# Embedding rows turned behind the first half tiles of the third output stage; the last stage's stores issued by SP, half a tile at a time

## What is computed

```python
def second_block(x, p, ...):
    h = x
    for i in range(DEPTH_2):                      # DEPTH_2 = 1
        xn = rms_norm(h, mix_norm[i])
        z = xn @ w_in[i]
        q, k, v, gate_a, u, gate_s = jnp.split(z, splits, axis=-1)
        attn = dilated_mixture_attention(q, k, v, q_norm[i], k_norm[i]) * jax.nn.silu(gate_a)
        ssm = s5_glu(u, ...) * jax.nn.silu(gate_s)
        h = h + jnp.concatenate([attn, ssm], axis=-1) @ w_out[i]
        gate = jax.nn.sigmoid(rms_norm(h, ple_norm[i]) @ w_ple_gate[i])
        h = h + gate * (p[i] @ w_ple_proj[i])
    return h
```

## Time and profile before

| | us |
|---|---|
| median of 3 runs | 2830.58 |
| lowest and highest run | 2827.45 and 2832.51 |
| the profiled execution, its own time | 2830.81 |
| span of that execution | 2829.0 |
| TensorE busy (PE) | 2726.1, 96% of the span |
| VectorE busy (DVE) | 1069.9, 38% |
| ScalarE busy (ACT) | 785.7, 28% |
| GpSimd busy (POOL) | 223.7, 8% |
| mean granted TensorE clock | 0.992 of full speed |

### The profile page before, as it was taken

One profiled execution on the slowest core, in us unless ns is written; L12 is line 12 of the kernel. 1 busy time (PEld: TensorE's weight loads), 2 busy tenths in 40 slices (PEclk: granted clock), 3 DMA queues, 4 the chain that ended last, 5 costly groups with the idle time before them and its releaser, 6 DMA issues. The chain is left out here.

```text
span 2829.0 us, 32445 instructions
## 1 busy us (share of the span) xinstructions
PE 2726.1 (96%) x12154; PEld 1529.1 (54%) x12154; DVE 1069.9 (38%) x3023; ACT 785.7 (28%) x1684; POOL 223.7 (8%) x409
## 2 busy tenths in 40 slices
PE   5999999999999999999999999999999999999998
PEld 3477544477644445466745476444654465644443
DVE  3257521299712223344400174123833473212211
ACT  3136400277711112322200264112211462111100
POOL 2000000000000000000060030200000002012000
PEclk8999999999999999999999999999999999999999
DMA  7030000012011220211010001333220204134311
GB/s 261 7 109 32 20 30 30 30 68 72 34 65 65 79 86 19 93 38 38 12 54 30 30 22 42 86 83 119 96 71 30 71 16 133 67 119 168 133 60 45
DMA packets 71867, 188.46 MB, mean 67 GB/s; under 512 B 6844, under 2 KB 9600, under 8 KB 70784
## 3 DMA queue, kind: packets, MB, share of 16 engines
q0 software_dynamic: 27808, 99.04, 10.8%
q1 hardware_dynamic: 43152, 86.97, 8.9%
q10 hardware_dynamic: 752, 0.38, 0.0%
HBM read 143.69 MB, written 43.01 MB: 66 GB/s over the span
## 5 line engine op out<-in xcount | busy, mean ns | idle before, releaser
L1305 PE MATMUL psum<-RW,hT 128*128 128x512 f32 (+2 forms) x2208 | 926.2, 575 | 7.5 <-ACT hT L2197 4.7
L1305 PEld LDWEIGHTS psum<-RW,hT 128*128 128x128 f32 x2208 | 428.0, 198 | 434.8 <-issue 412.8
L1271 PE MATMUL psum<-RW,RQ 128*128 128x512 f32 x832 | 362.3, 594 | 1.1 <-ACT RQ L2234 1.1
L1341 PE MATMUL psum<-RQ 64*128 64x256 f32 (+5 forms) x1344 | 291.7, 492 | 2.3 <-DVE small L2038 1.5
L2383 ACT ACTIVATE RP<-RP,small 128x1280 f32<-128x1280 f32 (+11 forms) x274 | 252.0, 920 | 131.0 <-DVE small L2038 127.0
L2038 DVE CUSTOM_DVE_ANT_0 RP<-psum,small 128x512 f32<-128x512 f32 (+1 forms) x382 | 201.5, 574 | 178.5 <-PE psum L1341 89.7
L1271 PEld LDWEIGHTS psum<-RW,RQ 128*128 128x128 f32 x832 | 157.0, 191 | 191.4 <-issue 191.4
L1353 PE MATMUL psum<-ident,RP 128*128 128x128 f32 x1388 | 203.7, 281 | 9.8 <-DVE RP L2051 4.5
L2395 ACT ACTIVATE RP<-psum 128x512 f32<-128x512 f32 (+1 forms) x288 | 150.1, 521 | 192.0 <-PE psum L1353 180.3
L1353 PEld LDWEIGHTS psum<-ident,RP 128*128 128x128 f32 x1388 | 149.4, 141 | 81.7 <-issue 67.9
L1341 PEld LDWEIGHTS psum<-RQ 64*128 64x128 f32 (+1 forms) x1344 | 139.2, 186 | 90.4 <-issue 48.9
(11 more groups left out here) (321 smaller groups left out, 2284.3 us busy)
## 6 DMA issues: line engine op xcount, KB each, us to landing
RW<-in_w_in SPq DMA_DIRECT2D x7, 2048.0 KB, 8.1
RW<-in_ev_w_in SPq DMA_DIRECT2D x6, 2048.0 KB, 8.1
RW<-in_od_w_ada SPq DMA_DIRECT2D x6, 2048.0 KB, 7.9
RW<-in_od_w_in SPq DMA_DIRECT2D x5, 2048.0 KB, 7.9
RQ<-in_ev_w_ada SPq DMA_DIRECT2D x4, 2048.0 KB, 21.0
RX<-in_x POOLq DMA_DIRECT2D x16, 512.0 KB, 6.0
y_even<-YR POOLq DMA_DIRECT2D x20, 256.0 KB, 2.3
RP<-y_even POOLq DMA_DIRECT2D x20, 256.0 KB, 3.0
```

The costliest lines, as they stand in the source:

```text
L1271: last = pe.matmul(main.bank(f), yT[:, kk, :], w_buf(n)[:, kk, :], start=kk == 0, stop=kk == KC - 1)
L1305: last = pe.matmul(main.bank(f)[:, 0:nc_], lhs_of(st["lhs"], j["t"], kk), w, start=kk == 0, stop=kk == kn - 1)
L1341: last = pe.matmul(main.bank(f)[:, 0:pc["w"]], q, kk[:, keys], start=i == 0, stop=i == len(u["qk"]) - 1)
```

## The change

The two loads get semaphores of their own: `s_p` for the embedding rows, `s_pw` for the projection's weights. The sixteen turns leave the state-space stage and stand in the third output stage, one group of four behind each of the jobs (0,0), (1,0), (0,1) and (1,1) (`turn_embedding`). ScalarE copies each group there. The wait for the projection's weights stands at the start of the last stage. The output is stored by SP in sixteen halves of 128 x 512, each as soon as VectorE has raised `s_ple` for it. POOL asks for the first three row tiles of the last stage ahead, and for each later one when both halves of the tile three before it are stored (`s_final`).

```diff
@@ -222,6 +222,8 @@
         s_prod = sem("gated_y_ready")
         s_out = sem("out_stored")
         s_p = sem("p_loaded")
+        s_pw = sem("embedding_weights_loaded")
+        s_final = [sem(f"final_rows{i}_stored") for i in range(3)]
         s_pad0 = sem("rpb_pad_stored")
         s_sq2 = sem("first_block_sum_ready")
         s_ple = sem("output_half_ready")
@@ -489,6 +491,7 @@
             for i, t in enumerate(tiles):
                 r["tiles"].append({"t": t, "m": [None, None], "x": new_x(), "xn": xn_count[0] + i, "rq": new_rms(),
                                    "rq2": new_rms() if kind == "final" else None, "at": i, "turned": None})
+            r["embedded"] = {}
             r["order"] = [(i, c) for i in range(len(tiles)) for c in range(2)]
             n = len(tiles)
             r["order"][1:3] = [(1, 0), (0, 1)]
@@ -499,6 +502,8 @@
                 if gated_here and c == 0 and i + 1 < len(tiles):
                     r["tiles"][i + 1]["turned"] = [turn.new("dve"), turn.new("act")]
                 r["tiles"][i]["m"][c] = weights[ws[c]]["last"] = main.new("dve")
+                if gated_here and i < 2:
+                    r["embedded"][i, c] = turn.new("act")
                 number_turns(r["jobs"].get((i, c), []))
             xn_count[0] += len(tiles)
             return r
@@ -680,12 +685,8 @@
         ssm["gt"] = [turn.new("act") for _ in range(8)]
         plan_gate()
         ssm["glu"] = [main.new("dve") for _ in range(8)]
-        ssm["pt"] = []
-        for _ in range(2):
+        for _ in range(4):
             plan_gate()
-        for _ in range(2):
-            plan_gate()
-            ssm["pt"] += [turn.new("act"), turn.new("act")]
         stages.append(ssm)
         stages.append(plan_out(io["w_out_2"][0], tokens, None, x_out, x_mix, "plain", 3, False, first_group, gated_here=True))
         gs = stages[-1]["groups"]
@@ -862,6 +863,13 @@
                     sp.dma_start(cos_t[:, :], io["k_cos"]).then_inc(s_tabs, 16)
                     sp.dma_start(sin_t[:, :], io["k_sin"]).then_inc(s_tabs, 16)
                     sp.dma_start(mask_window, io["k_mask_window"]).then_inc(s_tabs, 16)
+            for i, j in enumerate(ple["tiles"]):
+                for c in range(2):
+                    half = slice(512 * c, 512 * c + 512)
+                    sp.wait_ge(s_ple, 2 * i + c + 1)
+                    sp.dma_start(out[0, j["t"] * P:(j["t"] + 1) * P, half], x_slot(j["x"])[:, half]).then_inc(s_final[i % 3], 16)
+            for r in range(3):
+                sp.wait_ge(s_final[r], 32 * len(range(r, len(ple["tiles"]), 3)))
 
         @block.gpsimd
         def _(gp):
@@ -1091,22 +1099,17 @@
                     store_gate(st["gates"][12])
                     for j in out_mix["tiles"][1:3]:
                         load_y_and_gate(j)
-                    gp.dma_start(w_proj, kview(io["w_ple_proj_2"][0])).then_inc(s_p, 16)
+                    gp.dma_start(w_proj, kview(io["w_ple_proj_2"][0])).then_inc(s_pw, 16)
                     for e in st["gates"][13:]:
                         store_gate(e)
                 elif k == "ple":
                     ts = st["tiles"]
-                    for j, mixed in zip(ts[:2], out_mix["tiles"][5:7]):
-                        gp.wait_ge(s_xn, mixed["xn"] + 1)
+                    for i, j in enumerate(ts):
+                        if i < 3:
+                            gp.wait_ge(s_xn, out_mix["tiles"][5 + i]["xn"] + 1)
+                        else:
+                            gp.wait_ge(s_final[i % 3], 32 * (i // 3))
                         load_x(j, x_mix[j["t"] * P:(j["t"] + 1) * P, :])
-                    for i, j in enumerate(ts):
-                        gp.wait_ge(s_ple, 2 * i + 2)
-                        store_x(j, out[0, j["t"] * P:(j["t"] + 1) * P, :])
-                        if i + 2 < len(ts):
-                            load_x(ts[i + 2], x_mix[ts[i + 2]["t"] * P:(ts[i + 2]["t"] + 1) * P, :])
-            for i in range(3):
-                if xs_stored[i]:
-                    gp.wait_ge(s_xs[i], xs_stored[i])
 
 
         @block.tensor
@@ -1248,6 +1251,14 @@
                                 last = pe.transpose(turn.bank(f)[:, b * P:(b + 1) * P], y_tile(j["at"])[:, c0:c0 + P], ident[:, :])
                             turn.written(last)
 
+                    def turn_embedding(k, half, f):
+                        pe.wait_ge(s_p, 16)
+                        turn.wait_free(pe, f)
+                        for q in range(4):
+                            last = pe.transpose(turn.bank(f)[:, q * P:(q + 1) * P],
+                                                p_nat[:, 4 * half + q, k * P:(k + 1) * P], ident[:, :])
+                        turn.written(last)
+
                     if st["gated_here"]:
                         turn_product(ts[0])
                     for i, c in st["order"]:
@@ -1271,6 +1282,8 @@
                             last = pe.matmul(main.bank(f), yT[:, kk, :], w_buf(n)[:, kk, :],
                                              start=kk == 0, stop=kk == KC - 1)
                         main.written(last)
+                        if (i, c) in st["embedded"]:
+                            turn_embedding(i, c, st["embedded"][i, c])
                         turn_groups(st["jobs"].get((i, c), []))
                 elif k == "direct":
                     settle()
@@ -1489,21 +1502,11 @@
                         for kk in range(4):
                             last = pe.matmul(main.bank(f), glT[:, kk, s * P:(s + 1) * P], wglu[:, kk, :], start=kk == 0, stop=kk == 3)
                         main.written(last)
-                    for _ in range(2):
+                    for _ in range(4):
                         gate_job()
-                    for half in range(2):
-                        gate_job()
-                        pe.wait_ge(s_p, 32)
-                        for i in (2 * half, 2 * half + 1):
-                            f = st["pt"][i]
-                            turn.wait_free(pe, f)
-                            for q in range(4):
-                                last = pe.transpose(turn.bank(f)[:, q * P:(q + 1) * P],
-                                                    p_nat[:, 4 * (i % 2) + q, (i // 2) * P:(i // 2 + 1) * P], ident[:, :])
-                            turn.written(last)
-                    later.append((turn, st["pt"][-1]))
                 elif k == "ple":
-                    settle()
+                    pe.wait_ge(s_pw, 16)
+                    turn.wait_drained(pe, out_mix["embedded"][1, 1])
                     for j in st["tiles"]:
                         if j["needs"]:
                             wait_group(j["needs"])
@@ -2303,6 +2306,10 @@
                         j = st["tiles"][i]
                         if st["gated_here"] and c == 0 and i + 1 < len(st["tiles"]):
                             product_out(st["tiles"][i + 1])
+                        if (i, c) in st["embedded"]:
+                            f = st["embedded"][i, c]
+                            turn.wait_full(act, f)
+                            turn.consumed(fn(pT[i][:, 512 * c:512 * c + 512], turn.bank(f), ACT.Copy), f)
                         normed_groups(st["jobs"].get((i, c), []))
                         if c == 0:
                             continue
@@ -2479,14 +2486,8 @@
                     for s, f in enumerate(st["glu"]):
                         main.wait_drained(act, f)
                         fn(glu_slot(s), glu_slot(s), ACT.Sigmoid).then_inc(s_a, 1)
-                    for _ in range(2):
+                    for _ in range(4):
                         gate_out()
-                    for half in range(2):
-                        gate_out()
-                        for i in (2 * half, 2 * half + 1):
-                            f = st["pt"][i]
-                            turn.wait_full(act, f)
-                            turn.consumed(fn(pT[i // 2][:, 512 * (i % 2):512 * (i % 2) + 512], turn.bank(f), ACT.Copy), f)
                 elif k == "ple":
                     for j in st["tiles"]:
                         for c, (fg, fp) in enumerate(j["m"]):
```

## The result

The changed kernel takes 2815.6 us (median of 4 runs, 2810.91 to 2818.37). The kernel before took 2830.48 in the four runs beside it (2827.45 to 2832.51). The ratio is 0.9941, with a 95% interval of 0.9929 to 0.9953: faster, by 14.9 us, where 9.85 was forecast. The profiled execution took 2816.37, its span is 2814.4 (2829.0 before).

What follows compares the result with a forecast made beforehand. TensorE was taken to carry the time, with a 6.9 us wait for the projection's weights and a halved clock. -11.75 + 1.80 + 0.70 + 0.20 - 0.80 = -9.85 us gave 2820.7 us, range 2816.5 to 2825.

Steps and rivals of the forecast that it cites:

- to the first product of the out stage: Before the out stage: last gate job directly follows the third at full clock, first product at 2541.27 instead of 2553.02: -11.75 us.
- inside the out stage: Out stage: four groups of embedding turns come back, +1.80 us, and two waits for a bank, +0.70 us.
- start of the last stage to the last add: Start of last stage: the third row tile shares transfer engines with the second half of the last weights: +0.2 us.
- tail: After VectorE's last add: SP issues only a last half tile; -0.6 us for the smaller store, -0.2 for the issue: -0.8.
- T + 3.26: Start of out stage: first product comes 3.26 us after T, the last gate job's end, with ScalarE's chain ending last.
- The table load costs its row: Before the out stage: ScalarE's table load costs 1.28 us plus 0.02; rival that it is dearer, 2822.0, chance 0.05.
- the clock is not given back: Rival, argued for pauses at the out stage's start: another TensorE pause lowers the clock, 2.8 us return, 2823.5; chance 0.07.
- The stretch from the landing to the end of the span stays as it is.: Program's end, behind the last store's landing: the prediction assumed no change there and gave it no term.
- signs that the prediction named for being wrong: Out stage: first product starting later than 2543, or a new wait for a load, would show the forecast wrong.
- The tail gained: Rival at the end: SP's half stores land as late as POOL's whole ones or 0.5 later, 2821.5 to 2822; chance 0.07.
- the second half of the out stage's weights: Rival in the out stage: this load comes late and most of the gain is lost, near 2826; chance 0.06.
- the three slots: Rival in the last stage: slots refilled only after two SP stores land; hand-overs over 46 us cost time, near 2836; chance 0.02.

Runs made afterwards that it cites:

- e8: Changed kernel, but the embedding turns stay at their old place around the last gate job and wait for the rows alone: 2816.07 us.
- e2: Changed kernel with the old stores: POOL stores whole tiles and asks for two row tiles ahead, not three: 2821.16 us.
- a_again: The changed kernel run once more, unaltered, on another chip: 2818.14 us.
- e4: Changed kernel plus one line: POOL waits at its end until the last store has landed, issuing nothing more: 2821.7 us.
- e3: Changed kernel, but POOL issues the last of the sixteen half stores and waits for it: 2821.63 us.
- e5: Changed kernel, but SP stores whole tiles of 512 KB instead of halves: 2815.83 us.
- e1: Kernel before with only the SP half stores and three row tiles asked for ahead; embedding turns stay at their old place: 2823.53 us.

## Why the prediction was right and wrong

The sum again, by its own steps, profiled execution against profiled execution:

| step | forecast | measured | from |
|---|---|---|---|
| to the first product of the out stage | -11.75 | -11.67 | 2553.02 to 2541.35 |
| inside the out stage | +2.50 | +2.69 | 120.79 to 123.48 |
| start of the last stage to the last add | +0.20 | +1.94 | 144.42 to 146.36 |
| tail | -0.80 | -7.6 | 10.1 to 2.5 |
| sum | -9.85 | -14.6 | the spans, 2829.0 to 2814.4 |

**Before the out stage: right**, and for the reasons given. The job follows directly, the clock stays full, ScalarE's chain ends last, and the first product is at T + 3.26, as worked out. e8 shows the cause: with the wait for the rows alone, and nothing moved, the pause is gone. The table load costs its row (1.28) and no drain. By the Trainium skill ("ScalarE: Activation LUTs", section "What ACT_TABLE_LOAD costs"), as an estimate, the first product would have been 1.38 later; this case's rows don't agree with that part of the rule (0.02 us ahead of the load and 0.01 behind it).

**Inside the out stage: right.** The four groups cost 0.43 to 0.44 each (1.74). The two waits for a bank cost 0.48 each, where 0.35 was taken: from the gated turns to the next product it takes 1.35 with an embedding group ahead of them, and 0.87 in e8, which has none there.

**The start of the last stage: the term was mis-sized, and its reason was wrong.** It went by the third row tile, which e2 shows to matter little: without it the pause is the same. The pause grew by 0.34, which is no more than the two profiles of the changed kernel differ by (2.67 and 2.32), so the runs neither bear out the 0.20 nor refute it. The larger part, some 1.6, is the clock that fell behind the pause, and the sum had no term for it. The prediction held against that rival that "the pause of 2.33 us in the last stage left the clock at full". That row was true and proved little. In a_again the clock fell behind a pause of 2.32, and it did so behind all pauses of 2.1 to 2.7 in the kernels of this study, the kernel before alone excepted. One execution was taken as the rule. The rival "the clock is not given back" so came true in part, at another place than the one it was given for.

**The tail: this is the step that failed.** The sentence is "The stretch from the landing to the end of the span stays as it is." That stretch was some 6.7 us long (the store lands at 2819.36 + 2.9, near 2822.3, and the span ends at 2829.0), and I took it for a fixed cost of the program's end. 6.28 of it are POOL's drain, and the change took POOL off the end: what is left behind the landing is some 0.5 us (2813.9 to 2814.4). e4 shows it with the smallest edit, since a wait on POOL brings it back. e3 and e5 show that it is not the length of the stores, and e1 that the gain stands without the rest of the change. The terms that I did work out for the tail were near: 0.4 at the issue (0.2 taken), 0.9 at the landing (0.6 taken). Of the 0.9, half the size is 0.6 and the issuing engine 0.3, as e5 separates them (2.9 to 2.6 to 2.0). None of the signs that the prediction named for being wrong came (a first product later than 2543, a new wait for a load in the out stage): all of them lay on TensorE, and none on the tail.

**The other rivals** did not occur. The tail gained; the second half of the out stage's weights delayed nothing; and the three slots never came close to stopping the last stage. On where an SP store begins, the Trainium skill ("DMA: Bandwidth & Descriptors", section "Specifications") gives about 1 us to the first byte from GpSimd and 0.6 from sync, so 0.4 to SP. A 256 KB store landed after 2.0 us from SP and after 2.3 from POOL, so the trace agrees in direction, with 0.3; the prediction had taken nothing.

**What stays open.** Why the clock stayed full behind the pause of the kernel before wasn't found. There is one profile of that kernel, so it isn't shown either whether the change brought the loss of 1.6 or the kernel before has it in other executions too. Runs of one kernel differ by 3 to 9 us, and mostly the ones with the higher mean clock are the faster (the changed kernel: 0.996 at 2810.9, 0.994 at 2818.4). Which stretches upstream make this was not tried.

## What to carry to other kernels

Measure from the last instruction that computes to the end of the span, and account for all of it: here an engine's drain of 6 us stood there, to be had for nothing by letting another engine wait for the last store. A load that is waited for by itself gets a semaphore by itself; here that alone was worth the whole of TensorE's gain, and moving the work added nothing. Where a stage waits for weights, look at what else is on the DMA engines then, and ask for it after the weights if it isn't needed first, for a pause of TensorE can cost more than its length: 1.7 us more behind one of 2.3 here.

## What the runs showed of the hardware

- GpSimd's drain at the end of its block took 5.9 to 6.6 us in the profile of every kernel here, whether it had stored last, had only waited, or had been without transfers for 50 us. SP's took 7 ns in the kernels in which it stores the output, and 123 ns in the two in which its last act was a load. Neither the list of waits nor the chain shows POOL's.
- A pause of TensorE of 2.1 to 2.7 us brought the clock to half speed in the changed kernel (both times) and in e1 to e5 and e8, with jobs of 8.6 to 8.8 us instead of 7.0 in all of these. Behind the 2.33 of the kernel before it did not, nor behind pauses under 0.6. Each stretch at half clock was 3.4 us long. It began between 0.4 us before TensorE went on (e2) and 1.0 us after (e1), and the job was shorter by what of it fell into the pause (8.63 in e2, 8.83 in e1).
- SP issued a store 0.03 us after VectorE's end, POOL 0.44 and 0.30 after. 512 KB landed 2.6 us after the issue from SP and 2.9 from POOL, 256 KB after 2.0 and 2.3.
- 2 MB of weights landed after 12.1 us beside one store and two or three loads of 512 KB, after 10.0 beside the store, after 7.8 alone.
